# Transposes and scatter products one position earlier, a pair split and a result half by column halves, in the four-expert stage of a hybrid decoder kernel

## The reference

```python
def moe_swiglu(h, w_router, b_router, w_gate, w_up, w_down):
    t = h.reshape(nb * ns, d)
    logits = (t @ w_router + b_router).astype(F32)
    top_vals, top_idx = lax.top_k(logits, TOP_K)
    top_w = jax.nn.softmax(top_vals, axis=-1)
    gates = jnp.sum(jax.nn.one_hot(top_idx, N_EXPERTS, dtype=F32) * top_w[..., None], axis=1)
    out = jnp.zeros((nb * ns, d), F32)
    for e in range(N_EXPERTS):
        out = out + gates[:, e:e + 1] * swiglu(t, w_gate[e], w_up[e], w_down[e]).astype(F32)
    return out.reshape(nb, ns, d).astype(h.dtype)
```

## Time and profile before

| what | value |
|---|---|
| time of three runs, us | 1565.9, 1567.79, 1568.74 (median 1567.79) |
| profiled execution, us | 1563.69 |
| its span, first to last instruction, us | 1561.9 |
| PE busy | 1473.1 us, 94% |
| DVE busy | 1269.9 us, 81% |
| ACT busy | 1019.8 us, 65% |
| POOL busy | 217.2 us, 14% |
| PE in the chain of work that ended last | 78% |
| moved by DMA | 463.49 MB, 297 GB/s on average |

### The profile page before, as it was taken

How to read it: one execution, slowest core, us unless ns; L and a number is a source line. 1 busy time by engine, 2 the same in 40 slices (tenths; PEclk the granted TensorE clock), 3 DMA queues, 4 the chain that set the end, 5 groups by cost and what they waited for, 6 DMA issues and landing times.

```text
span 1561.9 us, 23262 instructions
## 1 busy us (share of the span) xinstructions
PE 1473.1 (94%) x8491; PEld 1237.6 (79%) x8491; DVE 1269.9 (81%) x1446; ACT 1019.8 (65%) x1105; POOL 217.2 (14%) x251
## 2 busy tenths in 40 slices
PE   6997899999798899999999999998999998988997
PEld 4776799999568777888888888887877877876885
DVE  4797677566885599889889889987997997997997
ACT  4556645555114577777767767766887877885884
POOL 0771146531590000000000000000000000000000
PEclk9998999999799999999999999999999999999999
DMA  9956376665484799999999999937999999996993
GB/s 312 321 186 212 109 266 227 232 232 205 152 281 153 264 338 353 367 341 360 373 350 357 360 356 357 352 108 282 356 386 350 365 350 336 365 390 251 399 400 118
DMA packets 231511, 463.49 MB, mean 297 GB/s; under 512 B 18287, under 2 KB 57719, under 8 KB 231415
## 3 DMA queue, kind: packets, MB, share of 16 engines
q1 hardware_dynamic: 229879, 461.55, 82.6%
q10 hardware_dynamic: 1536, 0.68, 0.2%
HBM read 461.15 MB, written 1.05 MB: 296 GB/s over the span
## 4 chain that ended last, share of the span: by engine, by line
PE 78%; DVE 10%; POOL 5%; ACT 2%; issue 2%; DMA 2%; SPq 1%; DVEq 0%; POOLq 0%; ACTq 0%
PE bank L2088 11%; PE bank L2455 9%; PE bank L2452 9%; PE bank L2449 9%; PE bank L2621 7%; PE bank L2624 7%; PE bank L2264 3%; PE bank L2559 2%; PE bank L2560 2%; PE bank L2567 2%; PE bank L2572 2%; PE bank L2571 2%; DVE bank L1431 2%; DVE wlo L1742 2%; PE bank L2640 2%
## 5 line engine op out<-in xcount | busy, mean ns | idle before, releaser
L1742 DVE TENSOR_TENSOR wlo<-ring,whi 128x2048 fp32r<-128x2048 f32 x168 | 381.6, 2288 | 49.4 <-PE bank L2455 45.8
L1070 ACT ACTIVATE whi<-ring 128x2048 fp32r<-128x2048 f32 x168 | 321.2, 1918 | 103.9 <-PE bank L2452 103.9
L1201 ACT ACTIVATE whi<-ring 128x2048 fp32r<-128x2048 f32 x168 | 319.3, 1919 | 66.4 <-PE bank L2567 33.9
L1898 DVE TENSOR_TENSOR wlo<-ring,whi 128x2048 fp32r<-128x2048 f32 x112 | 255.2, 2287 | 29.0 <-ACT whi L1201 28.7
L2452 PE MATMUL bank<-whi,xe_lo 128*128 128x512 f32 x448 | 175.0, 391 | 1.3 <-DVE wlo L1742 1.1
L2449 PE MATMUL bank<-whi,xe_hi 128*128 128x512 f32 x448 | 174.9, 390 | 0.0
L1349 DVE TENSOR_TENSOR ring_lo<-ring,ehi 128x2048 fp32r<-128x2048 f32 x45 | 106.3, 2362 | 61.9 <-ACT ehi L841 61.9
L1898 DVE TENSOR_TENSOR wlo_third<-ring,whi 128x2048 fp32r<-128x2048 f32 x56 | 128.0, 2286 | 11.9 <-ACT whi L1201 11.8
L2455 PE MATMUL bank<-wlo,xe_hi 128*128 128x512 f32 x448 | 119.9, 389 | 0.0
L2621 PE MATMUL bank<-whi,xs 128*128 128x512 f32 x336 | 97.6, 413 | 13.2 <-DVE hs L1855 12.4
L2452 PEld LDWEIGHTS bank<-whi,xe_lo 128*128 128x128 f32 x448 | 84.1, 188 | 20.6 <-DVE wlo L1742 3.4
(11 more groups left out here) (504 smaller groups left out, 2992.5 us busy)
## 6 DMA issues: line engine op xcount, KB each, us to landing
ring<-in_moe_w_gate_dram SPq DMA_DIRECT2D x112, 1024.0 KB, 7.1
ring<-in_moe_w_up_dram SPq DMA_DIRECT2D x112, 1024.0 KB, 7.0
ring<-in_moe_w_down_dram SPq DMA_DIRECT2D x112, 1024.0 KB, 7.2
ring<-in_mod_w_dram SPq DMA_DIRECT2D x24, 2048.0 KB, 9.7
ring<-in_ffn_w_gate_dram SPq DMA_DIRECT2D x11, 1024.0 KB, 6.6
ring<-in_ffn_w_up_dram SPq DMA_DIRECT2D x11, 1024.0 KB, 9.2
ring<-in_ffn_w_down_dram SPq DMA_DIRECT2D x11, 1024.0 KB, 5.0
ring<-in_conv_w_pw_dram SPq DMA_DIRECT2D x8, 1024.0 KB, 11.9
```

What stands on the lines that cost most here:

```text
L1070: act.activation(whi[:, n % HI_SLOTS, :], ring[:, s * HW:(s + 1) * HW], ACT.Copy).then_inc(hi_ready, 1)
L1201: act.activation(whi[:, q % HI_SLOTS, :], ring[:, s * HW:(s + 1) * HW], ACT.Copy).then_inc(hi_ready, 1)
L1742: v.tensor_tensor(wlo[:, n % LO_SLOTS, :], ring[:, s * HW:(s + 1) * HW], whi[:, n % HI_SLOTS, :].bitcast(F32), ALU.subtract).then_inc(lo_r ...
L1898: v.tensor_tensor(trio_lo(q), ring[:, s * HW:(s + 1) * HW], whi[:, q % HI_SLOTS, :].bitcast(F32), ALU.subtract).then_inc(lo_ready, 1)
```

## The change

Five edits, all in the interleaved stage.

- Wide gates are transposed once 12 products have passed since their end, not 20. That is one position earlier for each: for j = 1 to 6 from q = 30, 50, 66, 82, 100, 116 to 29, 49, 65, 81, 99, 115. Since two sets never share a position, small gates that stood behind move too: gates (1, 4), (1, 6), (2, 1), (2, 3) from 37, 51, 67, 84 to 36, 50, 66, 83.
- One pair of small halves goes from before to behind the wide half (0, G, 0, 1): that half moves from q = 11 to 9, and gate (1, 1) from 9, 10 to 10, 11. Wide gate 0 is transposed at 11 instead of 14, gate (1, 1) at 13 instead of 11. Its successor stays at q = 17.
- The planner's rule for small gates asks for a distance of four positions between transposes and the next gate, where it was three. The distances of three (gate (1, 0) to q = 9, (1, 4) to 40, (2, 3) to 87) are now four.
- The scatter groups of experts 1 and 2 go one position earlier on PE: behind q = 65 and 67, and behind 120 and 122. DVE's additions stay where they were.
- Position 120 has a function of its own, `wide_first_result`. It does all products of one column half before those of the other, so that it waits for the last gate (0, 6) only before the second; on the other hand it waits for the low part of its weights before its first product, where `wide_product` does so before its twelfth.

```diff
-PAIRS_AHEAD = ((0, 0, 2, 2, 2, 1, 2, 1, 2, 3, 1, 2, 1)
+PAIRS_AHEAD = ((0, 0, 2, 1, 3, 1, 2, 1, 2, 3, 1, 2, 1)
...
-TG_AT = transposes_at(G_ENDS, 20)
+TG_AT = transposes_at(G_ENDS, 12)
...
-        assert T_OF[_x] + 3 <= QBEGIN[_y] and T_OF[(_x[0], "U", _x[2])] + 1 <= QBEGIN[(_y[0], "U", _y[2])]
+        assert T_OF[_x] + 4 <= QBEGIN[_y] and T_OF[(_x[0], "U", _x[2])] + 1 <= QBEGIN[(_y[0], "U", _y[2])]
...
             def wide_steps(q, i, kind, j, h):
 
                 if kind == "D":
-                    if j == 0 and h == 0:
-                        pe.wait_ge(hl_ready, (i + 1) * FT)
-                        pe.wait_ge(sum_lo, GI[(0, FT - 1)])
                     c = [2 * h + d for d in range(2)]
...
+            def wide_first_result(q, i, kind, j, h):
+
+                pe.wait_ge(hi_ready, i * NH + (q + 1))
+                pe.wait_ge(hl_ready, i * FT + 1)
+                pe.wait_ge(sum_lo, GI[(0, 0)])
+                pe.wait_ge(wide_u, FT)
+                pe.wait_ge(row_sums, TI[(0, "U", FT - 1)])
+                pe.wait_ge(lo_ready, i * NH + (q + 1))
+                hi, lo = whi[:, q % HI_SLOTS, :], trio_lo(q)
+                parts, opens, closes = wide_steps(q, i, kind, j, h)
+                for s, (a_, b_, xh, xl, xt, at_) in enumerate(parts):
+                    if s:
+                        pe.wait_ge(hl_ready, (i + 1) * FT)
+                        pe.wait_ge(sum_lo, GI[(0, FT - 1)])
+                    for d, o in enumerate(at_):
+                        mm(a_[:, :], xh[d], hi[:, o:o + 512], start=d == 0, stop=False)
+                        mm(a_[:, :], xl[d], hi[:, o:o + 512], start=False, stop=False)
+                        ins = mm(b_[:, :], xt[d], hi[:, o:o + 512], start=d == 0, stop=False)
+                    if s:
+                        ins.then_inc(hi_used, 1)
+                    for d, o in enumerate(at_):
+                        mm(a_[:, :], xh[d], lo[:, o:o + 512], start=False, stop=False)
+                        ins = mm(b_[:, :], xt[d], lo[:, o:o + 512], start=False, stop=False)
+                ins.then_inc(lo_used, 1)
...
+                    elif (kind, j, h) == ("D", 0, 0):
+                        wide_first_result(q, i, kind, j, h)
                     elif q == NQ - 1:
...
-                        if q == SMALL_END[e] + 4:
+                        if q == SMALL_END[e] + 3:
                             small_scatter(e, 0, psum[SD[0]])
                             small_scatter(e, 1, psum[SD[1]])
-                        if q == SMALL_END[e] + 6:
+                        if q == SMALL_END[e] + 5:
                             pe.wait_ge(acc_half, e * NCOMB + 2)
```

## The result

| | before | after |
|---|---|---|
| median, us | 1566.9 (1565.9 to 1568.74, 4 runs) | 1543.57 (1540.09 to 1544.11, 4 runs) |
| profiled execution, us | 1563.69 | 1544.11 |
| first product of q=0, us from the start | 1050.86 | 1052.95 |
| first product of q=167 | 1543.80 | 1524.20 |
| stage, from the one to the other | 492.94 | 471.25 |

The ratio is 0.9855, 95% interval 0.984 to 0.987. The time was forecast at 1544.8 and the range at 1535 to 1557. The stage is 21.7 us shorter; the sum said 23.0. (The kernel before has one execution more here than in the table ahead of the prediction. The ratios of the first four experiments leave out one execution of it that took 2959.94 us.)

A forecast was written before the change was run, and what follows sets the result against it. PE bounds the stage, with DVE nearly as full, and PE's waits can be cut. Terms 4.7 + 4.7 + 0.5 + 3.5 + 9.2 + 0.4 = 23.0 us off the median 1567.79 give 1544.8; range 1535 to 1557.

The forecast's parts named there:

- Place A: q=9 to 17: the wait at q=9 and its clock fall go, a 3.0 us wait comes at q=17; -4.7 us.
- B, to 43: q=40: last step of gate (1, 4) one pass earlier, about 2 us of wait left, clock holds; -4.7 us.
- Place E: q=65 to 69: a new 2.6 us wait for hid_e replaces the old 2.20 for acc; -0.5 us.
- C, to 90: q=87: last step of gate (2, 3) one pass earlier, 2.8 us wait left, 1.7 of clock saved; -3.5 us.
- Place D: q=120 to 124: the 7.13 us wait for all hidden tiles goes, low pass 120 is late next; -9.2 us.
- The tail: Behind q=124: the 0.43 us idle at 1435.43 goes with the slack; -0.4 us.
- What bounds it: Interleaved stage, 1050 to 1548 us: short of PE, 473.6 us busy in 498; DVE nearly as full, 438.6.
- rival (1): Clock falls in the remaining waits, four of them at up to 2.5 us each: 10 us back, 1555; chance 0.23.
- (2): DVE is not the limit; ACT and DVE run further ahead and the waits vanish whole: 1535; chance 0.10.
- (3): Transfers become the bound late in the stage: 11 us back, 1556; chance 0.07.
- (4): Slower: PE reaches transposes before hid_e is made at all seven wide gates, clock falling in five: 1573; chance 0.03.
- (5): Only q=120 to 124 gains; waits at q=17, 40 and 87 stay as long as the old: about 1558; chance 0.04.

The follow-up runs named there:

- the first four experiments: Split pair, earlier wide-gate transposes, earlier scatter groups, new q=120 function, each alone on the kernel before: ratios 1.0002, 0.9959, 0.9969, 0.9970.
- the further edits: On the changed kernel: three gates' last steps ahead of their low passes, hid_e ahead of pass 66, late weight wait at q=120; all three together 1536.67 us.
- the split pair alone: Kernel before with only the second half of wide gate 0 moved to q=9, transposes as before: ratio 1.0002, stage +0.2 us.

## Why the prediction was right

By place, in us, measured from starts of positions counted from q=0:

| place | forecast | measured | waits forecast | waits measured |
|---|---|---|---|---|
| A, q=0 to 19 | -4.7 | -3.2 | 3.0 | 2.22, clock falls |
| B, to 43 | -4.7 | -4.7 | 2.0 | 1.59 |
| E, to 71 | -0.5 | -0.1 | 2.6 | 2.44 |
| C, to 90 | -3.5 | -3.5 | 2.8 | 2.22 |
| D, to 124 | -9.2 | -9.1 | 2.5 | 2.20, and 0.51 at q=118 |
| tail, to 167 | -0.4 | -1.0 | 0 | 0 |
| sum | -23.0 | -21.7 | | |

- **What bounds it** held. All waits that I named came, ended by the steps that I named, and no row is ended by hb.
- **Place A** is the term that missed. The start of q=17 was right, 4.9 us earlier against 4.7, and the 1.7 us lost behind it are the clock (6.0 x 0.28 in its window). That is the mechanism of rival (1), at one wait of the five instead of four. I had taken one row, the 2.20 us that kept the clock, for the behaviour at that size. The runs show a size at which it goes either way. The Trainium skill, "TensorE: Matmul & The Clock Gate", Part 1, that activity releases a default throttled state, was a better warning than my row: the windows at 0.72 behind 2.2 us agree with it, and those at 1.00 behind the same wait show that the fall need not come.
- **Waits too long by 0.2 to 0.8, starts right.** At q=40 and 87 the prediction's own terms say less than the waits that it names: 3.70 - 2.2 = 1.5 and 4.17 - 1.8 = 2.4, not 2.0 and 2.8. At q=17 the wait was the difference of two walks, DVE's to the step and PE's to the position, and DVE's decides the start. In the changed kernel q=0 began 2.09 us later than before, which is taken off here: I had PE there at 1101.1, and it came at 1106.06 - 2.22 - 2.09 = 1101.75; the start that DVE gave came at 1103.97 against a forecast of 1104.1.
- **Places B and C** were right in both terms, the pass of 2.2 us and the clock.
- **Place E** was right in kind. What I called a payback in a new place is bounded by three late things in a row, as the runs show: hid_e, then acc, then DVE's passes.
- **Place D** was right, start and end. The 0.51 us at q=118 I had missed, and it cost nothing, since DVE's pass 120 decides. The row names ACT, but DVE ended `hs`, which q=118 also waits for, in the same instant (1387.58 + 0.41, ACT's pass at 1386.07 + 1.94 = 1388.01); the wide gate's two steps, one pass earlier now, stand ahead of it:

```profile
1386.65 0.42 DVE L1832 TENSOR_TENSOR g_b<-bank,g_b 128x256 f32<-128x256 f32 x1
1386.98 0.68 DVE L1839 TENSOR_TENSOR hlW<-bank,hhW 128x512 fp32r<-128x512 f32 x1
1387.58 0.41 DVE L1855 TENSOR_TENSOR hs<-bank,hs 128x256 fp32r<-128x256 f32 x1
```

- **The tail** gave 1.0 and not 0.4: I counted the wait at q=127 alone. Before, positions 126 and 127 took 2.17 and 2.53 us from start to start, after the change 1.81 each: 1.1 us, which is all of it.
- **The time** missed by 1.2 us, and that it missed by no more is luck. It was forecast as the median of before less the sum, 1567.79 - 23.0 = 1544.8. With the stage as measured it would have been 1567.79 - 21.7 = 1546.1, against 1543.57: the median of three executions was high, and the sum, too large by 1.3, made up for half of it. With one execution more the median of before was 1566.9, and in the later sessions 1564.63, 1566.14 and 1564.35.
- **Rivals.** (2) was wrong: DVE's queue is what PE waits for. (3) does not hold for this kernel; its first signs come with a stage 4 to 8 us shorter. (4) happened at q=65 only; the further edits, which run DVE closer to its limit, brought it at q=49 too, with 0.48 and 0.84 us. (5) was wrong for the changed kernel, but the split pair alone behaved so.

## What to carry to other kernels

When an engine waits for a short step of a busy in-order engine, look what stands ahead of that step in the queue before counting load: here a step of 0.4 us stood behind a pass of 2.2 whose result nobody wanted yet, and swapping the two took a 2.2 us wait to 0.2. Follow each moved wait to the next late thing (the pair alone gained 4.7 us at q=9 and nothing at the end), and expect the edits not to add. Where total times scatter, count from a mark inside the program; it repeated to 0.1 us here where whole runs resolved 3.

## What the runs showed of the hardware

The granted clock behind a PE wait of 2.2 to 2.9 us fell in 9 of 23 cases, at a cost of some 1.5 to 1.7 us each, and equal waits at the same place differed between kernels (2.45 us fell, 2.44 did not). Removing other waits brought two falls that had not been there. With all waits at or below 1.6 us there was none. Half of the transferred bytes (182 GB/s instead of 361) left DVE busy for 437.5 us instead of 437.3 and ACT for 387.0 instead of 388.5.
